# Boundary between the two layers of a diffusion backbone: latent rows normalised first, context rows spread over the dense blocks behind

## The reference, cut to what matters

```python
h  = modulate(rms_norm(x,  g_mix[l]), sh1,  sc1)
hc = modulate(rms_norm(xc, g_mix[l]), csh1, csc1)
a_b, a_c, a_x, na_q, na_k, na_v, sw_q, sw_k, sw_v, ga, gb, gc = split_in(h @ w_in[l])
# the same projection of hc; attention of latents reads keys and values of hc
x = x + gt1 * merge_branches((o_a, o_b, o_c), (ga, gb, gc), w_branch[l], w_out[l])
x = x + gt2 * expert_choice_ffn(modulate(rms_norm(x, g_ffn[l]), sh2, sc2), ...)
# the same two updates of xc, in the first layer only
```

## Time and profile before

| | us |
|---|---|
| median of 3 runs | 1850.11 |
| lowest and highest run | 1849.13, 1851.18 |
| profiled execution | 1845.82 |
| its span, first to last instruction | 1843.7 |
| granted TensorE clock, mean over the span | 0.978 |

### The profile page before, as it was taken

The page is one execution under the profiler, slowest core; times in us unless marked ns, Lnnn a source line. Parts: engine busy times, 40 slices in busy tenths (PEclk is TensorE's granted clock), DMA queues, the critical chain, the costliest instruction groups (busy, mean ns, idle before and its releaser), DMA issues.

```text
span 1843.7 us, 26505 instructions
## 1 busy us (share of the span) xinstructions
PE 1688.7 (92%) x10846; PEld 980.3 (53%) x10846; DVE 773.4 (42%) x1751; ACT 476.2 (26%) x1047; POOL 110.0 (6%) x149
## 2 busy tenths in 40 slices
PE   6999999999998999999898799999999998777875
PEld 3887777776664333333232498877883333222222
DVE  3455556674434233333323665577743222111112
ACT  4224455552123100000000535555441000000001
POOL 1001210000001000000000102200000000000000
PEclk9999999999999999999999899999999999989998
DMA  9532322127779999999999765247889999999996
GB/s 352 156 91 74 104 80 70 35 81 257 263 275 363 410 428 427 428 428 427 427 428 428 259 194 146 75 132 262 283 307 426 425 426 424 425 424 425 424 424 287
DMA packets 153763, 543.83 MB, mean 295 GB/s; under 512 B 10218, under 2 KB 92592, under 8 KB 129324
## 3 DMA queue, kind: packets, MB, share of 16 engines
q1 hardware_dynamic: 150976, 535.87, 74.1%
q0 software_dynamic: 2400, 6.16, 1.2%
q10 hardware_dynamic: 268, 0.11, 0.0%
HBM read 539.13 MB, written 2.98 MB: 294 GB/s over the span
## 4 chain that ended last, share of the span: by engine, by line
PE 69%; DMA 23%; DVE 4%; ACT 2%; SPq 1%; issue 1%; POOL 0%; DVEq 0%; ACTq 0%
PE bank L2114 20%; PE bank L1975 12%; PE bank L1976 11%; PE bank L1977 11%; DMA ring<-in_w_exp_down 7%; DMA ring<-in_w_exp_gate 5%; DMA ring<-in_w_exp_up 4%; DMA spare<-in_w_exp_up 3%; PE bank L2027 2%; PE bank L2004 2%; PE bank L2088 2%; PE bank L1890 2%; PE bank L2014 2%; DMA split_slot<-in_w_exp_down 2%; DMA CONST<-in_w_exp_gate 2%; PE bank L2133 1%
## 5 line engine op out<-in xcount | busy, mean ns | idle before, releaser
L2114 PE MATMUL bank<-ring,XEP 128*32 128x256 f32 (+1 forms) x2352 | 381.4, 618 | 32.5 <-DMA ring<-in_w_exp_up 16.0
L1975 PE MATMUL bank<-HH,WH 128*128 128x512 f32 (+1 forms) x864 | 312.7, 362 | 5.3 <-DVE HL L1597 4.4
L1976 PE MATMUL bank<-HL,WH 128*128 128x512 f32 (+1 forms) x864 | 301.1, 348 | 0.0
L1977 PE MATMUL bank<-HH,WL 128*128 128x512 f32 (+1 forms) x864 | 300.6, 348 | 0.0
L2114 PEld LDWEIGHTS bank<-ring,XEP 128*32 128x32 f32 (+1 forms) x2352 | 113.5, 130 | 269.9 <-issue 221.9
L1568 DVE TENSOR_TENSOR WL<-ring,WH 128x1024 fp32r<-128x1024 f32 (+1 forms) x172 | 185.4, 1080 | 134.5 <-ACT WH L1347 133.7
L1822 DVE TENSOR_TENSOR X<-X,bank 128x512 f32<-128x512 f32 x192 | 119.0, 682 | 189.7 <-PE bank L2133 100.7
L1975 PEld LDWEIGHTS bank<-HH,WH 128*128 128x128 f32 x864 | 164.3, 190 | 54.5 <-issue 24.9
L2114 PE MATMUL bank<-ring,HIDT 128*32 128x256 f32 (+1 forms) x1232 | 156.3, 492 | 35.4 <-DMA ring<-in_w_exp_down 35.4
L1347 ACT CAST WH<-ring 128x1024 fp32r<-128x1024 f32 (+1 forms) x172 | 158.0, 927 | 101.9 <-PE bank L1977 64.7
L1977 PEld LDWEIGHTS bank<-HH,WL 128*128 128x128 f32 x864 | 164.7, 191 | 21.0
(11 more groups left out here) (231 smaller groups left out, 1949.3 us busy)
## 6 DMA issues: line engine op xcount, KB each, us to landing
ring<-in_w_exp_gate SPq DMA_DIRECT2D x55, 2048.0 KB, 30.8
ring<-in_w_exp_down SPq DMA_DIRECT2D x51, 2048.0 KB, 31.2
ring<-in_w_exp_up SPq DMA_DIRECT2D x48, 2048.0 KB, 32.7
ring<-in_w_ada SPq DMA_DIRECT2D x48, 1024.0 KB, 7.5
ring<-in_w_in SPq DMA_DIRECT2D x40, 1024.0 KB, 7.2
split_slot<-in_w_exp_up SPq DMA_DIRECT2D x9, 2048.0 KB, 27.8
ring<-in_w_in SPq DMA_DIRECT2D x28, 512.0 KB, 5.3
split_slot<-in_w_exp_down SPq DMA_DIRECT2D x7, 2048.0 KB, 37.7
```

The costliest lines, as they stand in the source:

```text
L1975: mm(t, wh, hi[:, k, 0:b.n], start=k == 0, stop=False)
L1976: mm(t, wh, lo[:, k, 0:b.n], start=False, stop=False)
L1977: last = mm(t, wl, hi[:, k, 0:b.n], start=False, stop=k == b.kk - 1)
L2114: last = mm(out_bank[tw * g:tw * g + tw, 0:nw], stationary(k), w[:, g::G] if spread else w[:, nw * g:nw * g + nw], start=k == 0, stop=k == ...
```

## The change

The norm of the second layer takes the latent tiles 0 and 1 alone, and the eight `trmod` steps that follow handle their 256 rows. The last expert's adds are reordered: DVE first makes the low half WL of the next layer's first block, then the adds of parts 0, 1, 4, 5 (the latents) and 2; parts 3, 6 and 7 become steps `late_add` among the `trmod` steps. The banks of the last scatter are permuted so that banks 0, 1, 2, 6 and 7 come free first. WL of the second block now stands ahead of the norm. The context tiles are squared by ACT at the end of ac2 and ac3, their norm (`which=1`) is a step behind ax0, and their eight `trmod` steps stand behind ax1 (two), ax2 (two), ax3 (two), ab0 (one) and ab1 (one). PE waits for 24 `ht_ready` before a block of 512 rows. The expert load into the spare memory waits for 24 as well and stands behind the two loads of nv.

```diff
+LATE_PARTS = (3, 6, 7)
@@ make_plan
-            P.add("norm", which=0, ntt=4)
+            P.add("norm", which=0, tiles=[0, 1])
...
+        def turn_steps(first, end, which=0, l=l):
+            tiles = [2 * which, 2 * which + 1] if l else [0, 1, 2, 3]
...
+        late_adds = [Step(kind="late_add", layer=l, i=i) for i in LATE_PARTS] if l else []
+        ctx_due = list(range(KD)) if l else []
...
-                    P.steps[l] += turns[:5]
+                    P.steps[l] += turns[:2] + late_adds[:1] + turns[2:4] + late_adds[1:2] + turns[4:5]
...
-                        P.steps[l] += turns[k + 5:k + 6]
+                        P.steps[l] += turns[k + 5:k + 6] + (late_adds[2:] if k == 0 else [])
...
                     run(ksteps(P, b) + [("done", b)])
+                    if l and name == "ac":
+                        P.add("square", tiles=[i])
+                    elif ctx_due and (name, i) == ("ax", 0):
+                        P.add("norm", which=1, tiles=[2, 3])
+                    elif ctx_due:
+                        n = 2 if name == "ax" else 1
+                        P.steps[l] += turn_steps(ctx_due[0], ctx_due[0] + n, 1)
+                        ctx_due = ctx_due[n:]
...
-        if last:
-            expert_load(Step(o_ready=("ht_ready", 2 * KD)))
...
         ch = col_chunk("nv")
+        if last:
+            expert_load(Step(o_ready=("ht_ready", 3 * KD)))
@@ scatter_banks, last expert
-            return ([GAB, UAB, XGB[0], XGB[1], HTB, SCB[0], SCB[1], YAB] if ns == 2 ...
+            return ([GAB, UAB, XGB[0], XGB[1], SCB[1], SCB[0], HTB, YAB] if ns == 2 ...
@@ scalar
+                    elif kind == "square":
+                        tt = s.tiles[0]
+                        act.wait_ge(x_added, ADD0[l] - ADDS[l - 1] + 2 * (tt + 1))
+                        square = nc.scalar.activation(XN[:, tt, :], X[:, tt, :], ACT.Square, accum_out=SS[:, tt:tt + 1])
+                        if tt == 3:
+                            square.then_inc(sq_ready, 1)
@@ vector
+                    elif kind == "late_add":
+                        add_part(ADD0[l - 1] + ADDS[l - 1] * (NE - 1), s.i, scatter_banks(NE - 1, 2)[s.i])
...
+                            if s.ns == 2 and e == NE - 1:
+                                low_half(next(step.blk for step in P.steps[l + 1] if step.kind == "k"))
+                                for i in (0, 1, 4, 5, 2):
+                                    add_part(a0, i, banks[i])
@@ tensor
+                        elif l and b.src == "h" and b.n == TOK and k == 0:
+                            pe.wait_ge(ht_ready, KD * (l + 2))
```

More of the change, by code:

```diff
@@ L405, in make_plan @@
             P.flush()
-            P.add("norm", which=0, ntt=4)
+            P.add("norm", which=0, tiles=[0, 1, 2, 3])
             ada(0, 2, pieces[2])()
@@ L415, in expert_load @@
             early.append(free)
-        def turn_steps(first, end, l=l):
-            return [Step(kind="trmod", layer=l, which=0, k=k, ntt=4, tile=P.tile(act=True), mods=P.mods, hts=8 * l + k) for k in range(first, end)]
+        def turn_steps(first, end, which=0, l=l):
+            tiles = [2 * which, 2 * which + 1] if l else [0, 1, 2, 3]
+            return [Step(kind="trmod", layer=l, which=which, k=k, tiles=tiles, tile=P.tile(act=True), mods=P.mods, hts=8 * (l + which) + k)
+                    for k in range(first, end)]
         turns = turn_steps(0, KD if l else KD // 2)
+        late_adds = [Step(kind="late_add", layer=l, i=i) for i in LATE_PARTS] if l else []
+        ctx_due = list(range(KD)) if l else []
         def col_chunk(name, l=l):
@@ L811, in make_plan @@
                 split(ahead[s.blk.b])
-            if s.kind == "norm" and l:
+            if s.kind == "norm" and l and not s.which:
                 early_split = [Step(kind="split", layer=l, blk=b, after_expert=last_in_slot(l - 1, ORDER[l - 1].index(NRING))) for b in layer_blocks[:2]]
-                out += early_split + [Step(kind="split_low", layer=l, blk=layer_blocks[0])]
+                out += early_split + [Step(kind="split_low", layer=l, blk=layer_blocks[1])]
             if s.kind == "trmod" and s.k == 0 and not l:
@@ L825, in make_plan @@
                     low()
-            if s.kind == "trmod" and s.k == KD - 1:
+            if s.kind == "trmod" and s.k == KD - 1 and not s.which:
                 split(layer_blocks[2])
@@ L1291, in norm @@
             def norm(s):
-                nc.scalar.activation(PRIME[:, 15 + norms[0]:16 + norms[0]], IDENT[:, 0:1], ACT.Sqrt)
-                for i in range(s.ntt):
-                    tt = i
+                if not s.which:
+                    nc.scalar.activation(PRIME[:, 14 + norms[0]:15 + norms[0]], IDENT[:, 0:1], ACT.Sqrt)
+                for tt in () if s.which else s.tiles:
                     if s.layer == DEPTH:
@@ L1303, in norm @@
                     last = nc.scalar.activation(XN[:, tt, :], X[:, tt, :], ACT.Square, accum_out=SS[:, tt:tt + 1])
-                last.then_inc(sq_ready, 1)
-                root(s)
+                if not s.which:
+                    last.then_inc(sq_ready, 1)
+                root(s.tiles)
                 if s.kind == "norm":
@@ L1372, in _ @@
                             act.wait_ge(ht_ready, s.hts - 1)
-                        for q in range(s.ntt // 2):
+                        for q in range(s.tiles[0] // 2, s.tiles[-1] // 2 + 1):
                             last = nc.scalar.activation(FT[s.k % 2][:, SEQ * q:SEQ * q + SEQ], BLK[s.tile.bank][:, SEQ * q:SEQ * q + SEQ], ACT.Identity,
@@ L1446, in _ @@
                         s.ntt = 2 * s.ns
-                        root(s)
+                        root(range(s.ntt))
                         act.wait_ge(logits_ready, l + 1)
@@ L1550, in finish_modulation, with low_half, add_part @@
                     nc.vector.tensor_tensor(m, m, gain, ALU.mult).then_inc(mod_ready, 1)
+            def low_half(b):
+                dve.wait_ge(split_hi, b.b + 1)
+                w = block_weights(b)
+                nc.vector.tensor_tensor(WL[b.buffer][:, 0:b.kk, :], w, WH[b.buffer][:, 0:b.kk, :].bitcast(f32),
+                                        ALU.subtract).then_inc(split_lo, 1)
+            def add_part(a0, i, bank):
+                j, q, c = i // 4, i // 2 % 2, i % 2
+                xs = X[:, 2 * q + j, 512 * c:512 * c + 512]
+                dve.wait_ge(sc_ready, a0 + i + 1)
+                nc.vector.tensor_tensor(xs, xs, bank[:], ALU.add).then_inc(x_added, 1)
             def by_column(bank):
@@ L1588, in _ @@
                     elif kind == "norm":
-                        norm(s.ntt)
+                        norm(s.tiles)
                         for c in range(2):
-                            for tt in range(s.ntt // 2):
+                            for tt in s.tiles[:len(s.tiles) // 2]:
                                 last = nc.vector.tensor_scalar(XN[:, tt, 512 * c:512 * c + 512], X[:, tt, 512 * c:512 * c + 512], RS[:, tt:tt + 1], None, ALU.mult)
@@ L1740, in _ @@
                         link(nc.vector.tensor_reduce(SS[:, 0:ntt], SSP[:, 0:ntt, :], AX.X, ALU.add))
-                        root(ntt)
+                        root(range(ntt))
                         lt = LGT[:, 0:ntt, :]
@@ L1811, in add_rows @@
                             banks = scatter_banks(e, s.ns)
-                            if s.ns == 2:
-                                parts = [(2 * q + j, c) for j in range(2) for q in range(2) for c in range(2)]
-                            else:
[L1815 to L1822, removed]
+                            if s.ns == 2 and e == NE - 1:
+                                low_half(next(step.blk for step in P.steps[l + 1] if step.kind == "k"))
+                                for i in (0, 1, 4, 5, 2):
+                                    add_part(a0, i, banks[i])
+                            elif s.ns == 2:
+                                for i in range(adds):
+                                    add_part(a0, i, banks[i])
+                            else:
+                                for c in range(adds):
+                                    xs, ys = X[:, 0:2, 256 * c:256 * c + 256], banks[c][:].rearrange("p (j n) -> p j n", j=2)
+                                    dve.wait_ge(sc_ready, a0 + c + 1)
+                                    nc.vector.tensor_tensor(xs, xs, ys, ALU.add).then_inc(x_added, 1)
                         def pick(n):
@@ L1864, in _ @@
                     elif kind == "final":
-                        norm(2)
+                        norm([0, 1])
                         dve.wait_ge(gf_in, 16)
@@ L1956, in _ @@
                         t = open_tile(s.tile)
-                        for tt in range(s.ntt):
+                        for tt in s.tiles:
                             last = nc.tensor.transpose(t[:, 128 * tt:128 * tt + 128], XN[:, tt, 128 * s.k:128 * s.k + 128], IDENT)
```

51 lines of the change are left out of this document (23 added, 28 removed).

## The result

The changed kernel took 1853.78 us in the median of 11 runs (1849.62 to 1857.24), the kernel before 1850.47 in 11 runs beside it: ratio 1.0019, 95% interval 1.0012 to 1.0027. That is 3.5 us slower (2.2 to 5.0): clear of noise, and under the 0.2% (3.7 us) that the chances called no difference, though the interval reaches beyond it. The forecast was 1852.0 with the larger chance on "same"; 1853.8 lies inside the range of 1845 to 1856.5 and just at the upper end of the forecast's own bounds, 1853.7.

What follows compares the result with a forecast made beforehand. The norm's chain, then DVE and PE together, bound the stretch before ac2, and PE the ten blocks behind it. Terms -6.4 + 6.8 + 1.2 + 0.2 = +1.8 took the median from 1850.1 to 1852; range 1845 to 1856.5.

Steps and rivals of the forecast that it cites:

- mechanism at ax2: Before ax2: squares, WH, WL and context norm delay emptying of ax1's bank, for which ax2 waits till about 15.9 behind ac2.
- ac2: Start of block ac2 after the eight latent `trmod` steps: 6.4 us earlier (5.4 to 7.5).
- the clock: From ax2 on: TensorE at half clock after the gap, at most 1.7 us, none if the clock stays; 1.2 taken.
- SP's queue: Weights of nq0/nk0 stand behind the 2 MB load gated by step 23; taken as just hidden, 0.
- signs that the prediction named for being wrong: ax2 within 2 us of ax1's end, nq0 waiting for WL with a DMA behind it, or ten blocks under 33 us.
- rival B: At nq0: weights late behind the load gated by step 23; +2.3 more, 1854.3, or 1856.3 if landing stretches; chance 0.16.
- first transpose: PE's first transpose after the second layer's norm, moved from 1042.68 to about 1040.3: 2.4 us earlier.
- ac2 to ax2: Stretch from ac2's start to ax2's start: ax2 at about 15.9 instead of 11.5, 4.4 us later.
- banks and transposes, up to nv0: From ax3 to nv0: 1.6 us for ax3 and ab0, 0.3 for later transposes, about 0.4 for ab3's bank wait.
- masks: POOL's masks leave the `trmod` stage, landing 2 to 10 behind ac2 beside WL of ax1 and ax2; 0.2 us with rounding.
- Rival A: Around ax2: spread steps vanish in DVE's idle share, ax2 not waiting for ax1's bank; -4.4 us, 1845.7; chance 0.17.
- Rival C: Before ac2: clock does not rise with the earlier transposes; gain 3.3 instead of 6.4, so +4.9, 1855; chance 0.12.

Runs made afterwards that it cites:

- Kernel 6: Changed kernel with context steps in own banks 3 and 4, expert load behind nq0's weights, and context squares behind WH: 1845.04 us, ratio 0.9977 to the kernel before.
- kernel 2: Changed kernel with context steps using banks 3 and 4 in turn instead of the round of three: 1848.02 us, ratio 0.9999 to the kernel before.
- kernel 3: Changed kernel with WH and WL of ax3 put ahead of the context norm: 1851.49 us, ratio 1.0010 to the kernel before.
- kernel 1: Changed kernel with the 2 MB expert load moved behind the load of nq0/nk0's weights in SP's queue: 1850.57 us, ratio 1.0004 to the kernel before.
- 7: Changed kernel with the three late adds back in front of the norm: 1855.68 us, ratio 1.0028 to the kernel before.
- kernel 4: Changed kernel without the second layer's context work, two ACT copies filling those columns, expert load waiting for 16 `ht_ready`: 1842.17 us, ratio 0.9957 to the kernel before.

## Why the prediction was right

The mechanism at ax2 held step by step, and the sum was short by 1.7 us. That it was no more is partly luck: ac2 came 1.2 earlier than forecast, the clock cost 1.1 more, and these two errors cancel. What is left is a term that the forecast had at nothing, SP's queue, with 2.1. Of the signs that the prediction named for being wrong, one did come: nq0 waits for WL with a DMA behind it; and nv0 stood 37.9 behind ac2, outside the 35 to 37 given. So what happened is the forecast's mechanism and rival B's together. Point by point, the forecast's terms against the two traces, up to the start of nq0 (minus is earlier):

```
term                                  forecast   measured
first transpose                         -2.4      -2.6
ac2                                     -6.4      -7.6
ac2 to ax2 (11.5 before)                +4.4      +4.2
clock at 1.2 GHz in ax2                 +1.2      +2.3
banks and transposes, up to nv0          +2.4   } +2.5
masks                                    +0.2   } with it
sum at nv0                              +1.8      +1.4
nq0 behind nv0                           0        +2.1
sum at nq0                              +1.8      +3.6
```

- **Up to ac2** the first transpose was right to 0.2 us. The 1.2 more won at ac2 have two parts. The clock was back 4.2 us after the first transpose, not after 5.9 as I carried over from the earlier trace rows; that is some 0.7. And my own sum for PE gave 1050.5, 18.1 behind the scatter, between which and the 1052 of a later clock I took 1051.0; that is the other 0.5. Kernel 6 shows the sum was good: there the clock came back 6.2 after the first transpose, and ac2 is at 18.14. The four kernels with the clock back earliest (3.9 to 4.6 after it) all have ac2 at 17.40 to 17.42, which is where the forecast had DVE alone (1049.9, 17.5): WL of ac2 ends at 1053.99 in the changed kernel, 17.3 behind the scatter, and ac2 starts at 1054.13. The windows show the clock's return in the changed kernel and in kernel 6, and the row is that WL:

```profile
1048.40:1048.60 0.20, 0.20 (x3) 0.20 (x3) 0.17 (x2) 0.14 (x1) 0.00 (x0) 0.65 0.76 266
1048.80:1049.20 0.40, 0.40 (x4) 0.40 (x4) 0.37 (x2) 0.40 (x1) 0.00 (x0) 0.77 0.37 131
1052.77 1.22 DVE L1574 TENSOR_TENSOR WL<-ring,WH 128x1024 fp32r<-128x1024 f32 x1
```

- **ax2** started 15.8 behind ac2, forecast 15.9, through the very order named: square, WH, WL, norm, WL, product, bank. Kernels 2 and 3 separate the bank from the place of WL, and both are needed for the wait.
- **The clock** fell at the end of that gap, and since ax2 was slow in whole, it cost 2.3 (6.01 from ax2 to ax3, against 2.88 + 0.35 + 0.45) rather than 1.2. I had bounded it by half of 3.4, the length of the slow stretch of the earlier trace rows; here the stretch was 6.8 us long, so the bound was too tight. In kernels 1 and 7 it was 3.4, and the cost 1.4 and 1.5, within the bound. That the fall comes with the wait for the bank is shown by kernel 2.
- **Masks** left the `trmod` stage as said and ran between 1.0 and 11.2 behind ac2 (2 to 10 was given), but met other work than I named. WL of ac3 and ax0 took 2.90 together instead of 2.44, and the root's first operation 0.37 instead of 0.16, both while POOL was at its masks; WL of ax1 and ax2 took their usual 1.22 and 1.23. Only the root lies on the path.
- **The term that was mis-sized is SP's queue.** I took it as "just hidden, 0" and held the rest as rival B. Step 23 came when forecast (53.7 behind the scatter, forecast 53.1 to 54.1), but from the expert load's issue to the landing of nq0's chunk it took 12.5 where I allowed 6.7 to 12.0, beyond the end of my own range, and every step on ACT behind the wait (the copy of nv0's result, for which PE's transposes waited 1.47) was late with it. Kernel 1 measures the term: 2.1, near rival B's 2.3.
- **Rival A** is refuted by the wait on the product in the profile, but it names what the repair is worth: kernel 2 is that rival made true, and with SP's queue mended as well the boundary gains 3.7. **Rival C** is refuted by ac2. That the head start alone is 7.4 to 8.0 and reaches the end, kernel 4 shows.

The median of runs, +3.3 by medians and +3.5 by ratio, agrees with the trace's +3.6 once the 4.3 us ahead of the last scatter are taken off. They belong to the two executions that were profiled: that of the kernel before, at 1845.82, was 4.6 below the median of its runs.

## What to carry to other kernels

When work is moved out of a chain into a stretch where PE never waits, read the queues there entry by entry: the idle share of an engine says nothing about where its next free place is, and here one WL and one bank in a round of three cost 2.5 us of waiting and, in the profiled execution, 2.3 us of clock, out of 7.6 won. A wait that is added to a DMA queue has to be priced by the next load behind it, with its landing, not by the load that waits; and where two loads share a semaphore, the first of them is as late as the second. And a second user of a rotating set of buffers changes the distance at which every old user meets itself.

## What was not expected of the hardware

- A gap of 4.2 us with 0.79 of small work in it brought TensorE from 2.4 to 1.2 GHz for more than a whole block: 24 matmuls of 256 columns took 5.29 us instead of 2.88. In kernel 1 the same gap (4.17) gave a mean of 0.67 over ax2 and its transposes, 5.12 us, so the price of one and the same wait ranges from 1.4 to 2.3. A gap of 1.8 us with the transposes in it (kernel 2), and one of about 3 us (kernel 3), left the clock up. Kernel 1's gap and ax2:

```profile
1066.10:1070.27 4.17, 0.63 (x5) 0.42 (x4) 2.68 (x7) 3.92 (x6) 0.00 (x0) 0.99 0.02 5
1070.27:1075.39 5.12, 5.04 (x28) 4.80 (x28) 2.75 (x6) 0.46 (x2) 0.00 (x0) 0.67 0.00 0
```

- The two loads of 512 KB issued behind the 2 MB, with the DMA engines otherwise idle (share 0.05 over ax3 to nv0), landed 8.4 and 11.1 us after their own issues; the two of 1 MB ahead of them landed after 5.0 and 7.1. In kernel 1, with the expert load out of the way, the same two loads of 512 KB, issued at 1061.2, took 5.2 (median). The loads issued behind nk0's half shared the engines with it, which may be why it came later than its place in the queue suggests; that was not tried.
